# RWKV head inverses two heads at a time on quarters of TensorE, with sparse attention woven through both stages

## What is computed

```
# mixer A, 6 heads of 64: a recurrence over the 512 tokens
sa = S @ a_t
S  = S * w_t + outer(sa, b_t) + outer(v_t, k_t)
y_t = S @ r_t
# mixer B, 6 heads of 64: attention in a latent of 128 over the keys that an index picked
logits = (q_lat * 64**-0.5) @ c.T          # masked by causality and by the top 128 keys of the index
o_lat  = softmax(logits) @ c
o      = o_lat @ w_uv[h]
```

## Time and profile before

| | us |
|---|---|
| median of 3 runs | 4778.43 (4777.96 to 4786.48) |
| the profiled execution, its time | 4777.99 |
| its span | 4776.1 |
| TensorE matmul busy in the span | 4288.1 (90%) |
| VectorE busy | 2803.2 (59%) |
| ScalarE busy | 2001.2 (42%) |

### The profile page before, as it was taken

The page is one execution under the profiler, slowest core; times in us unless marked ns, Lnnn a source line. Parts: engine busy times, 40 slices in busy tenths (PEclk is TensorE's granted clock), DMA queues, the critical chain, the costliest instruction groups (busy, mean ns, idle before and its releaser), DMA issues.

```text
span 4776.1 us, 53419 instructions
## 1 busy us (share of the span) xinstructions
PE 4288.1 (90%) x21514; PEld 3372.6 (71%) x21514; DVE 2803.2 (59%) x4627; ACT 2001.2 (42%) x3359; POOL 137.6 (3%) x123
## 2 busy tenths in 40 slices
PE   7899869995965679988999989899999998998998
PEld 5656658884754568876887677677877875776877
DVE  4466459994368479975445964444444468544444
ACT  3255448882323258873223333322332333233222
POOL 0000000000000000001000000000000000000000
PEclk9999969997988779998999988999999998899999
DMA  4334159992200089972222100122222221001221
GB/s 189 121 144 175 38 223 409 407 387 97 88 36 1 10 329 408 408 309 95 100 90 93 53 1 19 53 106 89 83 103 88 87 91 40 1 19 71 89 106 62
DMA packets 60671, 634.69 MB, mean 133 GB/s; under 512 B 6615, under 2 KB 6871, under 8 KB 25608
## 3 DMA queue, kind: packets, MB, share of 16 engines
q1 hardware_dynamic: 44872, 574.65, 30.6%
q0 software_dynamic: 8928, 32.51, 1.9%
q10 hardware_dynamic: 6624, 24.12, 1.2%
HBM read 600.80 MB, written 30.45 MB: 132 GB/s over the span
## 4 chain that ended last, share of the span: by engine, by line
PE 77%; DVE 15%; ACT 4%; DMA 2%; issue 1%; POOL 1%; DVEq 0%; POOLq 0%; SPq 0%; ACTq 0%
PE ps L345 13%; PE ps L346 13%; PE ps L347 13%; PE ps L1338 4%; PE ps L1337 4%; PE ps L1336 4%; PE ps L2882 3%; DVE wbuf_r L326 2%; PE ps L1354 2%; PE ps L1355 2%; PE ps L1356 2%; PE ps L993 2%; DVE arena L2541 1%; DVE arena L2539 1%; PE ps L975 1%
## 5 line engine op out<-in xcount | busy, mean ns | idle before, releaser
L346 PE MATMUL ps<-arena_r,wbuf_r 128*128 128x512 f32 x3104 | 1243.3, 401 | 0.0
L326 DVE TENSOR_TENSOR wbuf_r<-slot,wbuf_r 128x512 fp32r<-128x512 f32 (+1 forms) x832 | 586.6, 714 | 648.2 <-ACT wbuf_r L316 639.1
L345 PE MATMUL ps<-hT_r,wbuf_r 128*128 128x512 f32 x2144 | 866.1, 404 | 18.2 <-DVE arena_r L456 8.1
L347 PE MATMUL ps<-hT_r,wbuf_r 128*128 128x512 f32 x2144 | 851.9, 397 | 0.0
L316 ACT ACTIVATE wbuf_r<-slot 128x512 fp32r<-128x512 f32 (+1 forms) x832 | 507.3, 614 | 816.2 <-PE ps L347 680.4
L346 PEld LDWEIGHTS ps<-arena_r,wbuf_r 128*128 128x128 f32 x3104 | 586.8, 189 | 146.7 <-issue 4.6
L345 PEld LDWEIGHTS ps<-hT_r,wbuf_r 128*128 128x128 f32 x2144 | 404.5, 189 | 143.1 <-DVE arena_r L456 13.7
L347 PEld LDWEIGHTS ps<-hT_r,wbuf_r 128*128 128x128 f32 x2144 | 405.3, 189 | 100.7
L345 PE MATMUL ps<-arena_r,wbuf_r 128*128 128x512 f32 x960 | 384.9, 401 | 60.7 <-DVE arena_r L1161 60.7
L347 PE MATMUL ps<-arena_r,wbuf_r 128*128 128x512 f32 x960 | 383.6, 400 | 0.0
L345 PEld LDWEIGHTS ps<-arena_r,wbuf_r 128*128 128x128 f32 x960 | 183.2, 191 | 107.3 <-issue 62.8
(11 more groups left out here) (462 smaller groups left out, 7140.1 us busy)
## 6 DMA issues: line engine op xcount, KB each, us to landing
arena<-in_moe SPq DMA_DIRECT2D x82, 2048.0 KB, 10.0
slot<-in_moe SPq DMA_DIRECT2D x56, 2048.0 KB, 9.8
slot<-in_gu SPq DMA_DIRECT2D x44, 2048.0 KB, 7.7
slot<-in_ada SPq DMA_DIRECT2D x20, 2048.0 KB, 7.8
slot<-in_down SPq DMA_DIRECT2D x16, 2048.0 KB, 7.7
slot<-in_win SPq DMA_DIRECT2D x12, 2048.0 KB, 7.7
yrow<-arena ACTq DMA_DIRECT2D x46, 512.0 KB, 10.5
slot<-in_hgrn SPq DMA_DIRECT2D x8, 2048.0 KB, 7.7
```

The source lines that it names most:

```text
L326: v.tensor_tensor(lo[:, 0:w], src[:, off:off + w], hi[:, 0:w].bitcast(F32), ALU.subtract) \
L345: p.matmul(bank, hi[:, cs], rh[:, k, :], start=k == 0, stop=False, skip_group_check=True)
L346: p.matmul(bank, hi[:, cs], rl[:, k, :], start=False, stop=False, skip_group_check=True)
L347: t = p.matmul(bank, lo[:, cs], rh[:, k, :], start=False, stop=k == kt - 1, skip_group_check=True)
```

## The change

In the heads stage the unit is a pair of heads and no longer a head. Every product is cut to a 64 x 64 block, for one head and one chunk: 16 in place of the eight that two heads had of 128 x 128. The helper lists them (`BLOCKS`) so that consecutive ones lie in different quarters of the array: the row half is given by the partitions of the operands, the column half by those of the result. A result goes to one of two banks by its row half. The transpose of a level becomes a matmul with a 64 x 64 identity, in the same two banks as `AT`: ScalarE empties one, VectorE the other. All three pairs are in rotation at once, and each round also takes a step of mixer B (`beside=dsa`), whose remaining steps go on through the chunks stage. The heads stage and mixer B have banks of their own: `m.cps` (0 to 3), `m.dps` (4 to 6) and `m.ops` (7), where the heads had all eight.

In mixer B the scaling by 1/sum moves from the diagonal matrix to VectorE, which multiplies the tile of weights in place (`scale`); the turn becomes a plain transpose. In the chunks stage the outputs are formed in blocks of 64 too: 16 products of a chunk by itself (`own`) and 14 of the states (`past`), each added by VectorE separately. Five small copies (of masks and constants to the other half of the partitions) are added ahead of the heads in the first layer.

```
-                    t = p.transpose(bank[:, sl], TT[:, sl], ident)
-                four(("AT", i), (dve, n, "X", h, i), Ab, TT)
-                four(("TAT", i), (dve, n, "T", h, i), Tn, X1)
+        HALF = (slice(0, 64), slice(64, 128))
+        BLOCKS = [(t4, c, hh) for t4 in range(4) for c in range(2) for hh in range(2)]
+            for k in range(1, 6):
+                bank = take(("TX", k), lambda r: ((dve if r else act), n, "TX", i, k))
+                pe.wait_ge(*dve.at(n, "T", i, k - 1))
+                for t4, c, hh in BLOCKS:
+                    p.matmul(bank[c][HALF[hh], t4 * 64:t4 * 64 + 64], TT[HALF[c], hh, t4, :], ident[HALF[c], HALF[c]], start=True,
+                             stop=True, skip_group_check=True)
+                pe.wait_ge(*act.at(n, "A", i))
+                for t4, c, hh in BLOCKS:
+                    t = p.matmul(bank[c][HALF[hh], 256 + t4 * 64:256 + t4 * 64 + 64], A[HALF[c], hh, t4, :],
+                                 TT[HALF[c], hh, t4, :], start=True, stop=True, skip_group_check=True)
+                t.then_inc(*pe.mark(n, "TX", i, k))
                 yield
+                bank = take(("TAT", k), lambda r: (dve, n, "T", i, k))
+                for t4, c, hh in BLOCKS:
+                    t = p.matmul(bank[hh][HALF[c], t4 * 64:t4 * 64 + 64], TX[HALF[hh], c, 0, t4, :], TX[HALF[hh], c, 1, t4, :],
+                                 start=True, stop=True, skip_group_check=True)
...
+            def update(what, k, *key):
+                dve.wait_ge(*pe.at(n, *key))
+                for hh in range(2):
+                    v.copy_predicated(TT[:, hh], each(masks[:, k, 0:64], 4), quarter(ps.buf((what, i, hh)))) \
+                        .then_inc(*dve.mark(n, "T", i, k))
...
-                pe.wait_ge(*dve.at(n, "dsa factor", u))
+                pe.wait_ge(*dve.at(n, "dsa scaled", u))
                 for k in range(qt + 1):
-                    t = p.matmul(bank[:, k * 128:k * 128 + 128], pb[:, k * 128:k * 128 + 128], m.diag[u % 2], start=True,
-                                 stop=True, skip_group_check=True)
+                    t = p.transpose(bank[:, k * 128:k * 128 + 128], pb[:, k * 128:k * 128 + 128], ident)
...
-                v.tensor_scalar(m.diag[u % 2], ident, c[:, 4:5], None, ALU.mult).then_inc(*dve.mark(n, "dsa factor", u))
+                v.tensor_scalar(pb[:, 0:w], pb[:, 0:w], c[:, 4:5], None, ALU.mult).then_inc(*dve.mark(n, "dsa scaled", u))
...
-            in_turn(head_pe, p, m)
+            dsa = dsa_pe(p, m)
+            weave(*[head_pe(p, m, i) for i in range(3)], beside=dsa)
             edge(pe, m.name + " chunks")
-            weave(chunks_pe(p, m), dsa_pe(p, m))
+            weave(chunks_pe(p, m), dsa)
```

More of the change, by code:

```diff
@@ L2176, in weave @@
                         sides.remove(x)
+                if beside is not None:
+                    next(beside, None)
         def factors_pe(p, bank, sq, count, at):
@@ L2864, in rwkv_in_dve, with each @@
                 .then_inc(*dve.mark())
[L2867 to L2884, removed]
+        def each(x, n):
+            return x.unsqueeze(1).to_broadcast([128, n, 64])
@@ new lines, in build, with head_pe, take, of_heads @@
+        HALF = (slice(0, 64), slice(64, 128))
+        BLOCKS = [(t4, c, hh) for t4 in range(4) for c in range(2) for hh in range(2)]
+        def head_pe(p, m, i):
+            n = m.name
+            A, TX, ak = m.sets[i]
+            TT, Arb = m.TT[i], m.Arb[i]
+            def take(what, end):
+                bank = [m.cps.take((what, i, r), end(r)) for r in range(2)]
+                for r in range(2):
+                    for e in m.cps.before((what, i, r)):
+                        pe.wait_ge(*e)
+                return bank
+            def of_heads(what, end, lhs, rhs):
+                bank = take(what, end)
+                for t4, c, hh in BLOCKS:
+                    ts = slice(t4 * 128 + c * 64, t4 * 128 + c * 64 + 64)
+                    t = p.matmul(bank[hh][HALF[c], t4 * 64:t4 * 64 + 64], lhs[HALF[hh], i, ts], rhs[HALF[hh], i, ts],
+                                 start=True, stop=True, skip_group_check=True)
+                t.then_inc(*pe.mark(n, what, i))
+            of_heads("ba", lambda r: (dve, n, "T", i, 0), m.bh, m.ah)
@@ L2885, in head_pe @@
             yield
-            four("ab", (act, n, "A", h), ah, bh)
+            of_heads("ab", lambda r: (act, n, "A", i), m.ah, m.bh)
             yield
-            four("ka", (dve, n, "ka", h), kh, ah)
+            of_heads("ka", lambda r: (dve, n, "ka", i), m.kh, m.ah)
             yield
[L2890 to L2897, removed]
@@ L2915, in head_pe @@
                 yield
-            four("br", (dve, n, "br", h), bh, rh)
+            of_heads("br", lambda r: (dve, n, "br", i), m.bh, m.rh)
             yield
-            four("kr", (dve, n, "kr", h), kh, rh)
+            of_heads("kr", lambda r: (dve, n, "kr", i), m.kh, m.rh)
             yield
[L2920 to L2932, removed]
+            bank = take("y", lambda r: (act, n, "y", i))
+            pe.wait_ge(*dve.at(n, "kr", i))
+            for t4, c, hh in BLOCKS:
+                h = 2 * i + hh
+                t = p.matmul(bank[c][HALF[hh], t4 * 64:t4 * 64 + 64], m.vtok[HALF[c], t4, h * 64:h * 64 + 64],
+                             ak[HALF[c], hh, t4, :], start=True, stop=True, skip_group_check=True)
@@ L2950, in head_act @@
             yield
[L2951 to L2959, removed]
+            act.wait_ge(*pe.at(n, "y", i))
+            for c in range(2):
+                a.activation(y_blocks(m.y[i])[:, :, c, :], quarter(ps.buf(("y", i, c))), ACT.Copy) \
+                    .then_inc(*act.mark(n, "y", i))
@@ new lines, in head_dve, with masked @@
+        def head_dve(v, m, i):
+            n, ps = m.name, m.cps
+            A, TX, ak = m.sets[i]
+            TT, Arb = m.TT[i], m.Arb[i]
+            def masked(dst, what, mask, *key):
+                dve.wait_ge(*pe.at(n, what, i))
+                for hh in range(2):
+                    v.tensor_tensor(dst[:, hh], quarter(ps.buf((what, i, hh))), each(mask[:, 0:64], 4), ALU.mult) \
+                        .then_inc(*dve.mark(*key))
+            def update(what, k, *key):
+                dve.wait_ge(*pe.at(n, *key))
+                for hh in range(2):
+                    v.copy_predicated(TT[:, hh], each(masks[:, k, 0:64], 4), quarter(ps.buf((what, i, hh)))) \
+                        .then_inc(*dve.mark(n, "T", i, k))
+            v.tensor_copy(TT.rearrange("p b t v -> p (b t) v"), each(us[:, 64:128], 8)).then_inc(*dve.mark())
@@ L2977, in head_dve @@
                 yield
-            dve.wait_ge(*pe.at(n, "br", h))
-            v.tensor_tensor(by4(m.Arb[h]), by4(m.ps.buf(("br", h))), m4(ui), ALU.mult).then_inc(*dve.mark(n, "br", h))
+            masked(Arb, "br", ui, n, "br", i)
             yield
-            dve.wait_ge(*pe.at(n, "kr", h))
-            v.tensor_tensor(by4(ak), by4(m.ps.buf(("kr", h))), m4(ui), ALU.mult).then_inc(*dve.mark(n, "kr", h))
+            masked(ak, "kr", ui, n, "kr", i)
             yield
-        def in_turn(head, e, m):
-            for h0 in (0, 3):
-                group = [head(e, m, h0 + i) for i in range(3)]
-                while group:
-                    for x in list(group):
-                        try:
-                            next(x)
-                        except StopIteration:
-                            group.remove(x)
@@ L3169, in mix_act @@
             edge(act, m.name + " heads")
-            in_turn(head_act, a, m)
+            dsa = dsa_act(a, m)
+            weave(*[head_act(a, m, i) for i in range(3)], beside=dsa)
             edge(act, m.name + " chunks")
-            weave(chunks_act(a, m), dsa_act(a, m))
+            weave(chunks_act(a, m), dsa)
             rwkv_norm_act(a, m)
@@ L3178, in mix_dve @@
             edge(dve, m.name + " heads")
-            in_turn(head_dve, v, m)
+            dsa = dsa_dve(v, m)
+            weave(*[head_dve(v, m, i) for i in range(3)], beside=dsa)
             edge(dve, m.name + " chunks")
-            weave(chunks_dve(v, m), dsa_dve(v, m))
+            weave(chunks_dve(v, m), dsa)
             rwkv_norm_dve(v, m)
```

148 lines of the change are left out of this document (85 added, 63 removed).

## The result

The changed kernel takes 4667.69 us (median of 4 runs, 4662.26 to 4675.34) against 4782.45 us (4777.96 to 4793.27, 4 runs) of the kernel before beside it: a ratio of 0.9758, with a 95% interval from 0.9735 to 0.9781. It is 115 us faster. The forecast was 4686 with a range from 4632 to 4735. The profiled execution took 4668.77 us, its span is 4666.9: 109.2 us less than the 4776.1 of before.

What follows compares the result with a forecast made beforehand. TensorE was taken as full in the heads. Heads 98 and chunks 63 us save 48 us in the first layer and 45 in the second; less one for copies, 92 off 4777.99 gives 4686, range 4632 to 4735.

Steps and rivals of the forecast that it cites:

- I take 0.021, 44 us: TensorE in the new heads: 0.021 us a record, between bounds 0.0145 and 0.029, so 44 us for 2112 records.
- Only two at a time: Rival: two quarters work at once, 0.029 us a record, heads 109 us, 4708 in all; chance 0.20.
- Four quarters at full pace and light waits: Rival: records at 0.0145 us, doubles of 9 us, heads 76, chunks 59, 4635 in all; chance 0.17.
- double round: Heads: a TX and a TAT round of the levels with their woven steps; five such doubles take 61 us.
- The seven other rounds: Heads rounds outside the levels: takes 2.0, woven 1.8, mask wait 1.1, so 4.9 us each, 34 us.
- half of its 10 us of cold start: Second layer: slower clock made its heads 10 us longer; half stays, so 211.3 less 166, 45 us gained.
- The clock rival: Rival: waits between small matmuls keep TensorE at 1.2 GHz; with two thirds cold, 4832 us; chance 0.04.
- the chain: Chunks stage: the last four chunks run alone, each step waiting on the one before, 4.2 us a chunk, 17 us.
- The 3 us set aside for the clock: Chunks stage: 3 us added to 60, since TensorE works less than half of the time in the chain.
- The quarters don't overlap: Rival: 0.058 us a record, 122 us for 2112, 21 us slower a layer, 4820 in all; chance 0.02.
- The weave stalls: Rival: each woven step holds TensorE 1.5 us more for masks, exponentials or banks, 51 us, 4737; chance 0.08.
- The 3 us for the array's change from 128 rows to 64: Heads: after each of 17 woven steps the array returns to 64 rows, 0.2 us each, 3 us.

Runs made afterwards that it cites:

- The heads alone: Changed kernel without the weave in the heads, all 29 steps of mixer B in the chunks stage: 4681.96 us, ratio 0.9785.
- quarter_runs: Changed kernel with its 16 blocks reordered, four blocks (eight records) of one quarter after each other, then four of the next: 4764.39 us.
- mask_first: Changed kernel with VectorE's part of each woven step in the heads placed before its part of the three pairs: 4655.89 us, ratio 0.9729.
- the last two kernels: VectorE's woven step first plus TT turned by 8 transposes, against the changed kernel: 4653.82 us; that with a woven step every second heads round: 4649.82 us.

## Why the prediction was right, and where its sizes were off

**The direction and the stages.** Heads 93.8 and 97.0 us for 98, within its ends of 88 and 109; chunks 59.8 and 56.0 for 63, the second just under its lower end of 57; a layer 153 for 161 and 166. The 17 steps in the heads are there, TensorE's turns wait for the mask in most rounds, and the chunks give back what the steps and the turn took. The profiled execution is 17 us below the forecast: 20 in the two layers, less 3 outside (4 us lost there, 1 was allowed for).

**The price of a record (the step "I take 0.021, 44 us") was mis-sized.** In a burst it is 0.0135, no more than the lower bound of 0.0145; from take to take it is 0.015 to 0.017. *Only two at a time* has fallen as a mechanism. The Trainium skill, TensorE: Matmul & The Clock Gate, section "Wait — 56ns, not 53.3ns?", states a floor of some 25 ns between starts; the 32 records in 0.69 us are 13.5 ns apart on the mean, so on four quarters it does not hold, and the measurement decides. *Four quarters at full pace and light waits* had the first half right and the second wrong, so its 4635 was not reached either.

**A term was missing: the supply of instructions.** The sum priced TensorE's array and its waits, and no row of the kernel before could show a limit of a supply that was asked for one packet in some 14 us. At 128 records in 3.7 us the sustained price is 0.029, the very number of the rival that fell, from another cause. The heads alone show it bare. In the woven heads it is a small cause: the gap of 1.21 us within a take is the one long gap in the matmuls of the first layer's heads that is put down to issue, and 360 records fewer gave 4 us a layer.

**The rounds.** The TX rounds of after start at 2827.47, 2838.02, 2851.91, 2864.10 and 2875.19, and the levels end at 2889.26: 12.4 us a double round on the mean, where the forecast had 12.2 at 0.021 and 10.7 at 0.0145. That the mean came out right at the wrong price is luck: two errors nearly cancelled. The five doubles by themselves, with the granted clock behind the busy times:

```profile
2827.47:2838.02 10.55, 8.70 (x306) 6.75 (x306) 7.09 (x17) 4.83 (x13) 0.00 (x0) 1.00 0.01 3
2838.02:2851.91 13.89, 11.02 (x312) 8.98 (x312) 6.82 (x17) 4.12 (x11) 0.00 (x0) 0.88 0.02 4
2851.91:2864.10 12.19, 9.71 (x308) 6.95 (x308) 7.07 (x17) 4.98 (x14) 0.00 (x0) 1.00 0.01 3
2864.10:2875.19 11.09, 9.24 (x312) 7.44 (x311) 6.82 (x17) 4.12 (x11) 0.00 (x0) 1.00 0.02 5
2875.19:2889.26 14.07, 11.61 (x312) 8.00 (x314) 7.09 (x17) 5.60 (x15) 0.00 (x0) 0.87 0.01 2
```

The three at full clock take 11.3 us on the mean, not far from 10.7, with the mask's waits in them (10 us of the stage are won back without these). The two of 13.9 and 14.1 us are those in which the clock fell; in the first of them lies the supply's gap as well. So the mask's waits, the clock and, least, the supply took the place of the records' price. The seven other rounds took 93.84 - 61.8 = 32 us for 34 and 3.

**VectorE** had 52 us of work for the forecast's 62, so it is no bound; that the mask came late was its order, not its load. The forecast named the wait and did not ask whether the order could remove it.

**The second layer** gained 58 us, not 45. The forecast left half of its 10 us of cold start in place. The heads there had a mean clock of 0.91, much like the 0.90 before, but a stretch at 1.2 GHz costs what TensorE's work in it costs, and that is now less.

**The clock rival** was seen in small. In the heads the mean clock was 0.95 and 0.91, which is about 10 us of the 94 at 1.2 GHz, in two stretches, and at most an estimated 5 us of time, if all work in them took twice as long. The first follows on the waits of 1.21 and 1.13 us in the timeline above. In the last chunks, where TensorE has only the chain, it was seen again:

```profile
2937.30:2941.90 4.60, 3.57 (x57) 2.79 (x53) 0.99 (x3) 0.48 (x1) 0.00 (x0) 0.82 0.00 0
2941.90:2947.79 5.89, 4.86 (x54) 3.92 (x53) 0.97 (x3) 0.49 (x1) 0.00 (x0) 0.50 0.01 3
2947.79:2952.86 5.07, 3.30 (x41) 2.74 (x39) 0.99 (x3) 0.48 (x1) 0.00 (x0) 0.50 0.00 0
```

These are three chunks of the chain, from U (L3065) to U: 4.6 us while part of it still ran at 2.4 GHz, then 5.9 and 5.1 at 1.2 GHz, for 4.2 in the forecast. The 3 us set aside for the clock cover that.

**The quarters don't overlap** was refuted by the timeline of after, and quarter_runs shows the price had they been issued in runs: most of the gain gone, 4764. **The weave stalls** set 1.5 us for each woven step, 51 us in all; the mask's waits that could be won back were 10 us a layer, 0.6 a step.

**Left open.** What moves the time outside the two stages by several us from run to run (the heads start between 2811 and 2824 us in these kernels) was not looked into, nor why the gains of mask_first and of the last two kernels are smaller in the whole time than in their windows. The 3 us for the array's change from 128 rows to 64 were not measured by themselves. Of the chunks' 10 us without the weave, the turn measures 8.2 a layer when undone over both stages of the woven kernel; the outputs in blocks of 64 were not tried by themselves. Whether a packet of instructions could come sooner wasn't tried.

## What to carry to other kernels

A product cut into four blocks for the quarters of the array pays when its zeros were computed before, and when neighbours in the program lie in different quarters; but each block is two records and two weight loads that must be fetched, so price it by records too, here 128 in 3.7 us. Work woven between takes is worth only the idle time it fills: look whose result the next product waits for, and put that result first in its engine's queue, which here was worth 10 us a layer by the windows, where the weave as it stood was worth 5 (in the whole time, 12 and 14 us for both layers, the two don't differ). Measure the weave and what it is woven into apart.

## What the runs showed of the hardware that was not expected

- TensorE's instructions arrive in packets of 16.4 KB, 255 instructions, some 3.7 us apart when they are used up as fast as they come: 3.71, 3.74 and 3.65 us a packet in the first layer of three kernels whose heads had nothing between, and no two packets closer than 3.37. Short matmuls use one up sooner, and the gap shows as "issue".
- Four quarters of 64 x 64 take 32-bit records 0.0135 us apart within 32 of them, each quarter at the same 0.060 as alone.
- TensorE starts matmuls past ones that wait for a busy quarter, within a short reach (three records in the rows of quarter_runs): from take to take 0.015 to 0.017, 0.018 and 0.036 us a record for the three orders of the same 16 blocks.
- A transpose with 64 partitions and 128 stationary columns, into all 128 partitions of a bank, works in the half of the rows: 8 records in 0.46 us.
